# Five masked score levels of a gated linear-attention mixer, each computed as two 64-key halves instead of one 128-key product

## The chip, the cores and the metric

One NeuronCore of one Trainium2 chip runs the whole program. The metric is the device time of one execution in microseconds (us). Three executions of the kernel before took 3752.68, 3755.21 and 3758.10 us; their median, 3755.21 us, is the time before.

## What is computed

The program is a stack of four residual layers over 1024 tokens of 1024 channels. Only one part of the first layer matters here, its second mixer (a gated linear attention with 8 heads of 128 key and 128 value channels). Per head it computes, for gate decays `g` summed along the tokens:

```
g_c    = cumsum(log_f) within a chunk
scores = sum_d q[t,d] * k[s,d] * exp(g[t,d] - g[s,d])      for s <= t, else 0
out    = scores @ v + (q * exp(g)) @ state
state  = state * exp(g_end) + (k * exp(g_end - g))^T @ v
```

The reference uses chunks of 64 tokens; the kernel uses chunks of 128, which gives the same result. Before it stands a recurrent mixer, behind it an output projection, and behind that a second layer (a delta-rule recurrence) and two layers of attention, retention and pooling. None of them is touched.

## The kernel before, in words

`hgrn2` (from L529) runs the second mixer. All five engines run programs of their own and meet at semaphores. The work goes head by head: head 0, then a loop over heads 1 to 6, then head 7, all with the same `head` function on each engine.

**The levels.** `exp(g[t]-g[s])` can't be taken for a whole chunk as a product of a factor of t and a factor of s, for it would overflow. So the score matrix of a chunk (keys on the 128 partitions, queries along the free axis) is put together from five levels. For levels 0 to 3 the chunk is cut into blocks of 64, 32, 16 and 8 tokens (`HG_CROSS`), and the level holds the scores of keys in an even block with queries in the odd block right behind it, both decayed to the border between the two. Level 4 holds the scores inside blocks of 8 (`HG_DIAG`). Each level goes through four stations:

- `distance` (VectorE, L812 to L825): differences of `g` into `E`.
- `decays` (ScalarE, L704 to L712): exponentials of `E`.
- `decayed` (VectorE, L835/L837 for levels 0 to 3, L841/L842 for level 4 and for the state's operands): keys times decay into `ke`, queries times decay into `qe`. For levels 0 to 3 `qe` holds the queries of odd blocks alone, packed: 64 for each chunk. `ke` and `qe` have two buffers each, taken in turn.
- `level` (TensorE, L593 to L607): 8 float32 products, one for each chunk of 128 tokens, at L603. The stationary operand is the chunk's 128 keys of `ke`, the moving one the chunk's 64 packed queries (128 at level 4). The result goes to one PSUM bank per level (two at level 4, `B0`). A float32 product is two weight loads and two passes in the trace, so a level is 16 loads and 16 passes.
- `take_level` (VectorE, L851, L855): the scores that the level's mask marks are copied into `st`. Scores outside the mask are computed by the product and thrown away.

**The order on TensorE** within a head is written out by hand. The projections of the next head stand between the levels:

```
project_f(h+1); norm(h-1)
level(h,0); level(h,1)
project_q(h+1)
level(h,2); level(h,3)
project_g(h+1)
level(h,4); turn_k(h); state_steps(h)
project_v(h+1)
output(h)
```

`project_f`, `project_q` and `project_g` are 48 float16 products of 512 columns each (L142), `project_v` 192 of 128 columns (L157). `norm` (L637) sums squares of the previous head's output, `turn_k` (L613) transposes keys, `state_steps` (L621) forms what each chunk adds to the state, `output` (L629, L630) forms the head's output. `state_steps` waits for ScalarE's copy of the turned keys (L746) and for VectorE's take of level 4 (L855). `head(7)` has no projections, and `head(0)` has no norm of a head before it.

ScalarE takes in order: the decays of levels 0 and 1, `rstd(h-1)` (L716, L718, released by `norm`), the decays of level 2 (L704), `high_part(h-1)` (L722), `take_f(h+1)` (L679 with a table load, L680, and a weight split L109), a table load, the decays of level 3 (L704), then those of level 4 (L706 to L708) and of the state (L710 to L712), then `take_q(h+1)` (a table load and L686), `take_g(h+1)` (L690), the copy L746, `take_v(h+1)` (L694). `take_q` waits for VectorE to be done with the old queries (L907).

VectorE takes in order: the distances and decayed operands of levels 0 and 1, a copy of v (L885), take of level 0, the decayed operands of level 2, `normed(h-1)` (L860, L862), the distance of level 3, take of level 1, the decayed operands of level 3 (L835, L837), a low part (L868), the distances of level 4 and the state (L819 to L825), a weight split (L115), take of level 2, the decayed operands of level 4, take of level 3, the decayed operands of the state (L841, L842), `take_q` (L803), take of level 4 (L855), `take_g` (L807), the chain of states (L919, L922).

Of the kernel before, what the change touches and what calls it, by code (L numbers as in the profile page):

```python
# [130 lines left out]
def channel_major(pe, K, slot, rnd, u_hi, u_lo, banks, tile_ready=None):  # L131

    pe.wait_ge(K.w_full[slot], rnd + 2)
    w_hi = K.w_hi[:, slot, :].rearrange("p (k c) -> p k c", k=KT)
    w_lo = K.w_lo[:, slot, :].rearrange("p (k c) -> p k c", k=KT)
    for half, bank in enumerate(banks):
        cols = slice(half * HALF, (half + 1) * HALF)
        for k in range(KT):
            if half == 0 and tile_ready is not None:
                pe.wait_ge(tile_ready, k + 1)  # L140
            for n, (w, u) in enumerate(((w_hi, u_hi), (w_hi, u_lo), (w_lo, u_hi))):
                last = pe.matmul(K.psum[:, bank, :], w[:, k, :], u[:, k, cols],  # L142
                                 start=(k == 0 and n == 0), stop=(k == KT - 1 and n == 2))
    last.then_inc(K.w_free[slot], 1)


def token_major(pe, K, slot, rnd, u_hi, u_lo, banks):

    pe.wait_ge(K.w_full[slot], rnd + 2)
    w_hi = K.w_hi[:, slot, :].rearrange("p (k c) -> p k c", k=KT)  # L150
    w_lo = K.w_lo[:, slot, :].rearrange("p (k c) -> p k c", k=KT)
    for t in range(TT):
        toks = slice(t * P, (t + 1) * P)
        out = K.psum[:, banks[t // 4], (t % 4) * P:(t % 4 + 1) * P]
        for k in range(KT):
            for n, (w, u) in enumerate(((w_hi, u_hi), (w_hi, u_lo), (w_lo, u_hi))):
                last = pe.matmul(out, u[:, k, toks], w[:, k, :],  # L157
                                 start=(k == 0 and n == 0), stop=(k == KT - 1 and n == 2))
    last.then_inc(K.w_free[slot], 1)
# [369 lines left out]
def hgrn2(nc, K, A, first_round, ahead, spare):  # L529
# [7 lines left out]
    with nc.cleanup_on_exit(), ExitStack() as c:  # L537
# [7 lines left out]
        qe, ke = sb("qe", [P, 2, S]), sb("ke", [P, 2, S])  # L545
# [19 lines left out]
        A0, A1, B0, B1 = (K.bank_pair(n) for n in range(4))  # L565
        in_chunks = lambda x: x.rearrange("p (c t) -> p c t", c=NC)
        side = lambda x, n, late_side: x.rearrange("p (n a b) -> p n a b", a=2, b=HG_CROSS[n])[:, :, late_side, :]
        cross = lambda n: in_chunks(K.psum[:, 4 + n, :])
        later = lambda n: in_chunks(qe[:, n % 2, 0:S // 2])
        flat_states = states[:, :, :].rearrange("p c n -> p (c n)")  # L570

        with nc.Block() as block:
            @block.sync
            def _(sp):
                sp.dma_start(masks[:, :, :], A["c_hg_masks"]).then_inc(consts_in, 16)
                weight_loads(sp, K, first_round, H, lambda h: hgrn2_units(A, h), ahead)

            @block.tensor
            def _(pe):
                def project_f(h):  # L580
                    pe.wait_ge(g_taken, h + 1)
                    channel_major(pe, K, 0, h + first_round, K.u_hi, K.u_lo, (0, 1))

                def project_q(h):
                    pe.wait_ge(v_ready, h + 1)
                    channel_major(pe, K, 1, h + first_round, K.u_hi, K.u_lo, (2, 3))

                def project_g(h):
                    pe.wait_ge(f_ready, h + 1)
                    channel_major(pe, K, 2, h + first_round, K.u_hi, K.u_lo, (0, 1))  # L590

                def project_v(h):
                    pe.wait_ge(q_taken, h + 1)  # L593
                    token_major(pe, K, 3, h + first_round, K.u_hi, K.u_lo, (2, 3))

                def level(h, n):
                    pe.wait_ge(qk_ready, h * 6 + (n + 1))
                    if n == 2:
                        pe.wait_ge(rstd_ready, h + 1)
                    elif n == 4:  # L600
                        pe.wait_ge(level_taken, h * 5 + 2)
                    for ch in range(NC):
                        last = pe.matmul(cross(n)[:, ch, :] if n < 4 else in_chunks(B0)[:, ch, :],  # L603
                                         in_chunks(ke[:, n % 2, :])[:, ch, :],
                                         later(n)[:, ch, :] if n < 4 else in_chunks(qe[:, n % 2, :])[:, ch, :],
                                         start=True, stop=True)
                    last.then_inc(level_done, 1)  # L607

                def turn_k(h):
                    pe.wait_ge(qk_ready, h * 6 + 6)  # L610
                    pe.wait_ge(level_taken, h * 5 + 4)
                    for ch in range(NC):
                        last = pe.transpose(in_chunks(B1)[:, ch, :], in_chunks(ke[:, 1, :])[:, ch, :],  # L613
                                            K.ident[:, :])
                    last.then_inc(kt_done, 1)

                def state_steps(h):
                    pe.wait_ge(kt_ready, h + 1)
                    pe.wait_ge(level_taken, h * 5 + 5)
                    for ch in range(NC):  # L620
                        last = pe.matmul(in_chunks(B0)[:, ch, :], in_chunks(late[:, :])[:, ch, :],  # L621
                                         v[:, ch, :], start=True, stop=True)
                    last.then_inc(ds_done, 1)

                def output(h):
                    pe.wait_ge(state_ready, h + 1)
                    for ch in range(NC):
                        out = in_chunks(B1)[:, ch, :]
                        pe.matmul(out, v[:, ch, :], st[:, ch, :], start=True, stop=False)  # L629
                        last = pe.matmul(out, states[:, ch, :], in_chunks(qe[:, 1, :])[:, ch, :],  # L630
                                         start=False, stop=True)
                    last.then_inc(o_done, 1)

                def norm(h):
                    pe.wait_ge(o_ready, h + 1)
                    for half in range(2):
                        last = pe.matmul(B1[:, half * HALF:(half + 1) * HALF], K.ones[:, :],  # L637
                                         flat_states[:, half * HALF:(half + 1) * HALF], start=True, stop=True)
                    last.then_inc(norm_done, 1)

                def head(h, previous, following):
                    if following:
                        project_f(h + 1)
                    if previous:
                        norm(h - 1)
                    level(h, 0)
                    level(h, 1)
                    if following:
                        project_q(h + 1)
                    level(h, 2)  # L650
                    level(h, 3)
                    if following:
                        project_g(h + 1)
                    level(h, 4)
                    turn_k(h)
                    state_steps(h)
                    if following:
                        project_v(h + 1)
                    output(h)

                project_f(0)
                project_q(0)
                project_g(0)
                project_v(0)
                head(0, False, True)
                with pe.Fori(0, H - 2) as i:
                    head(i + 1, True, True)
                head(H - 1, True, False)
                norm(H - 1)
# [2524 lines left out]
```

## Time and profile before

| | |
|---|---|
| median of 3 executions | 3755.21 us |
| the profiled execution, its own time | 3758.37 us |
| its span in the trace | 3756.6 us |
| TensorE busy over the span | 90% (3394.3 us) |
| TensorE weight loads | 56% |
| VectorE, ScalarE, GpSimd busy | 50%, 37%, 15% |
| mean granted TensorE clock | 0.954 of full |
| the second mixer in the span | from about 320 to 839 us |
| busy time of L603 (the levels), 8 heads | 87.2 us of 640 passes |

In the profile PE is TensorE's matmul side, PEld its weight loads, DVE VectorE, ACT ScalarE. PEclk is the granted TensorE clock as a share of full speed: 1.00 is 2.4 GHz, 0.50 is 1.2 GHz. The shapes of a PE row are rows*columns of the array that the stationary operand takes, then the moving operand.

### The profile page before, as it was taken

The page shows a single profiled execution, that of the slowest core. Times are in us where ns is not written, and L with a number is a line of the kernel's source. Part 1 is how long each engine was busy: PE and PEld are TensorE (multiplying, and loading weights), DVE is VectorE, ACT ScalarE, POOL GpSimd, SP SyncE. Part 2 cuts the span into 40 slices and gives each one's busy share as a digit, 9 for nine tenths or more (in the row PEclk, how much of TensorE's full clock was granted, in tenths as well). Part 3 has the DMA queues.
Part 4 walks back from the last instruction along what each step waited for, and adds up shares of the span by engine and source line. Part 5 has one row for each costly group of instructions (what it writes and reads, how often), then busy time and mean ns, then how long its engine had stood idle before and what let it go on. Part 6 is the DMA issues. An engine that isn't in the chain of part 4 may idle for free. (4 is left out here: it accounts for less than half of the span.)

```text
span 3756.6 us, 74433 instructions
## 1 busy us (share of the span) xinstructions
PE 3394.3 (90%) x32138; PEld 2113.8 (56%) x32138; DVE 1872.9 (50%) x2563; ACT 1408.1 (37%) x2026; POOL 548.9 (15%) x350
## 2 busy tenths in 40 slices
PE   6887999969899898999998999979899999889889
PEld 3334766654444345888887457646544566657434
DVE  3654566653344724544554546654352366744342
ACT  3553354432355532323333435542311255523211
POOL 3000000002000002323332032300060133100330
PEclk8998999979999999999999999999999999999999
DMA  5101011103225643111110221011012111020121
GB/s 163 33 22 50 28 39 30 38 10 136 64 75 119 142 115 100 62 43 62 43 62 8 96 74 40 23 48 31 30 47 73 57 45 34 1 61 24 46 75 45
DMA packets 308334, 215.36 MB, mean 57 GB/s; under 512 B 125411, under 2 KB 283950, under 8 KB 305454
## 3 DMA queue, kind: packets, MB, share of 16 engines
q1 hardware_dynamic: 307608, 210.70, 18.7%
q8 instruction: 240, 3.93, 0.4%
q10 hardware_dynamic: 442, 0.37, 0.0%
q14 instruction: 44, 0.36, 0.0%
HBM read 173.26 MB, written 41.98 MB: 57 GB/s over the span
## 5 line engine op out<-in xcount | busy, mean ns | idle before, releaser
L142 PE MATMUL psum<-u,w_hi 128*128 128x512 f16 x2816 | 855.7, 386 | 103.1 <-DVEq L798 32.0
L142 PE MATMUL psum<-u,w_lo 128*128 128x512 f16 x1408 | 542.1, 385 | 0.0
L142 PEld LDWEIGHTS psum<-u,w_hi 128*128 128x128 f16 x2816 | 278.6, 100 | 452.6 <-issue 55.5
L97 POOL TENSOR_TENSOR w_hi<-stage,w_scale 128x1024 f16<-128x1024 f32 x52 | 99.4, 1912 | 1247.6 <-PE psum L142 604.8
L1063 PE MATMUL psum<-w_hi,merged 128*128 128x512 f16 x768 | 236.6, 390 | 25.0 <-PEq L2909 9.0
L115 DVE SCALAR_TENSOR_TENSOR w_lo<-stage,w_hi 128x1024 f16<-128x1024 f32 x124 | 149.1, 1219 | 184.6 <-ACT w_hi L109 184.5
L2497 DVE CUSTOM_DVE_ANT_0 probs_att<-psum,bias_att 128x1024 f32<-128x1024 f32 x128 | 156.7, 1224 | 168.3 <-PE psum L2309 167.5
L2287 PE MATMUL psum<-u,w_hi 128*128 128x512 f16 x768 | 231.7, 384 | 6.7 <-PEq L966 6.7
L142 PEld LDWEIGHTS psum<-u,w_lo 128*128 128x128 f16 x1408 | 139.8, 99 | 172.6 <-issue 11.5
L1063 PE MATMUL psum<-held_hi_out,merged 128*128 128x512 f16 x768 | 231.1, 379 | 0.0
L157 PE MATMUL psum<-w_hi,u 128*128 128x128 f16 x2048 | 173.2, 219 | 0.0
L157 PE MATMUL psum<-w_lo,u 128*128 128x128 f16 x1024 | 172.3, 219 | 0.0
L2119 DVE COPY_PREDICATED Tt_rc<-tmask_rc,psum 128x256 f32<-128x256 uint32 x192 | 83.4, 443 | 173.7 <-PE psum L1804 156.0
L142 PE MATMUL psum<-mix_b_rp,w_hi 128*128 128x512 f16 x512 | 153.7, 382 | 11.3 <-DVE mix_b_rp L1569 10.8
L157 PEld LDWEIGHTS psum<-w_hi,u 128*128 128x128 f16 x2048 | 157.9, 98 | 4.9 <-issue 4.6
L2406 ACT ACTIVATE probs_att<-probs_att,neg_max_att 128x1024 f32<-128x1024 f32 x128 | 146.3, 1146 | 19.6 <-DVE neg_max_att L2501 19.4
L2337 PE MATMUL psum<-turned_att,merged 128*128 128x128 f32 x1024 | 139.7, 281 | 15.0 <-ACT sq_att L2420 14.6
L1063 PE MATMUL psum<-w_lo,merged 128*128 128x512 f16 x384 | 149.6, 390 | 0.0
L2337 PEld LDWEIGHTS psum<-turned_att,merged 128*128 128x128 f32 x1024 | 132.4, 195 | 27.7 <-issue 17.7
L109 ACT ACTIVATE w_hi<-stage 128x1024 f16<-128x1024 f32 x124 | 127.6, 1048 | 52.1 <-PE psum L1063 41.2
L1063 PEld LDWEIGHTS psum<-w_hi,merged 128*128 128x128 f16 x768 | 76.8, 100 | 124.7 <-issue 38.8
L2287 PE MATMUL psum<-u,w_lo 128*128 128x512 f16 x384 | 146.8, 382 | 0.0
(446 smaller groups left out, 6842.2 us busy)
## 6 DMA issues: line engine op xcount, KB each, us to landing
stage<-w_in SPq DMA_DIRECT2D x72, 512.0 KB, 3.8
X<-rwkv_chunks SPq DMA_DIRECT2D x14, 1792.0 KB, 8.4
stage<-ab_w_in SPq DMA_DIRECT2D x48, 512.0 KB, 4.9
stage<-rw_w_in SPq DMA_DIRECT2D x32, 512.0 KB, 4.4
rwkv_chunks<-work_rp SPq DMA_DIRECT2D x26, 512.0 KB, 5.7
stage<-w_out SPq DMA_DIRECT2D x24, 512.0 KB, 5.8
X<-x SPq DMA_DIRECT2D x16, 512.0 KB, 10.8
stage<-ab_w_out SPq DMA_DIRECT2D x16, 512.0 KB, 5.5
```

Of the source, the lines that this page charges most:

```text
L97: pool.tensor_tensor(K.w_hi[:, slot, :], K.stage[:, slot, :], scale, ALU.mult).then_inc(K.w_half[slot], 1)
L109: act.mul(K.w_hi[:, slot, :], K.stage[:, slot, :], W_SCALE).then_inc(K.w_half[slot], 1)
L115: dve.scalar_tensor_tensor(K.w_lo[:, slot, :], K.stage[:, slot, :], W_SCALE, K.w_hi[:, slot, :], ALU.mult, ALU.subtract).then_inc(K.w_full ...
L142: last = pe.matmul(K.psum[:, bank, :], w[:, k, :], u[:, k, cols], start=(k == 0 and n == 0), stop=(k == KT - 1 and n == 2))
L157: last = pe.matmul(out, u[:, k, toks], w[:, k, :], start=(k == 0 and n == 0), stop=(k == KT - 1 and n == 2))
L1063: last = pe.matmul(bank_of(half, t), m[:, 2 * u + k, toks(t)], w[:, at, w_cols], start=(u == 0 and k == 0 and n == 0), stop=(u == UH - 1 a ...
L2119: dve.copy_predicated(Tt[:, q, g * GJ:g * GJ + GJ], mask, data).then_inc(t_ready, 1)
L2287: last = pe.matmul(K.psum[:, PROJ + half, :], w[:, kt, :], u[:, kt, cols(half)], start=(kt == 0 and n == 0), stop=(kt == KT - 1 and n == 2))
L2337: last = pe.matmul(K.psum[:, O_BANK, (i % 4) * P:(i % 4 + 1) * P], v_tiles[h % 2][:, half * 4 + n, :], turned[:, half, n, :], start=(half ...
L2406: act.activation(probs[:, s % 2, m, :], probs[:, s % 2, m, :], ACT.Exp, bias=neg_max[:, s % 2, m:m + 1], accum_out=sums[:, s % 2, m:m + 1] ...
L2497: dve.tensor_tensor_reduce(probs[:, s % 2, m, :], K.bank_pair(m), bias[:, h % 2, at:at + S], LOGIT_UNSCALE, LOWEST, ALU.add, ALU.max, neg_ ...
```

## The change

Only `level` on TensorE changes. Level 0 multiplies the first 64 keys of a chunk alone (the later 64 are in no even block of 64 tokens) with the chunk's 64 packed queries, into PSUM partitions 0 to 63. Levels 1 to 3 become two products for each chunk: keys 0 to 63 with the first 32 packed queries into partitions 0 to 63, and keys 64 to 127 with the last 32 packed queries into partitions 64 to 127. Level 4 becomes two products as well, 64 keys with the 64 queries of their own half. Banks, masks, semaphores and everything on the other engines stay. The numbers of products are 8, 16, 16, 16, 16 where they were 8 in each level.

```
@@ def level(h, n) @@
+                    keys = in_chunks(ke[:, n % 2, :])
+                    queries, out = (later(n), cross(n)) if n < 4 else (in_chunks(qe[:, 0, :]), in_chunks(B0))
                     for ch in range(NC):
-                        last = pe.matmul(cross(n)[:, ch, :] if n < 4 else in_chunks(B0)[:, ch, :],
-                                         in_chunks(ke[:, n % 2, :])[:, ch, :],
-                                         later(n)[:, ch, :] if n < 4 else in_chunks(qe[:, n % 2, :])[:, ch, :],
-                                         start=True, stop=True)
+                        if n == 0:
+                            last = pe.matmul(out[0:64, ch, :], keys[:, ch, 0:64], queries[:, ch, :],
+                                             start=True, stop=True)
+                            continue
+                        width = 32 if n < 4 else 64
+                        for side_of in range(2):
+                            at, cols = slice(64 * side_of, 64 * side_of + 64), slice(width * side_of,
+                                                                                    width * side_of + width)
+                            last = pe.matmul(out[at, ch, cols], keys[:, ch, at], queries[:, ch, cols],
+                                             start=True, stop=True)
                     last.then_inc(level_done, 1)
```

## Rows read from the trace of the kernel before

**Rows 1.** Heads 3, 5, 7: length; busy PE, PEld, DVE, ACT, POOL; PEclk; DMA; GB/s

```profile
533.20:594.40 61.20, 59.10 (x479) 41.01 (x477) 38.80 (x50) 29.35 (x30) 0.00 (x0) 1.00 0.12 34
655.60:718.00 62.40, 60.64 (x478) 41.82 (x476) 38.76 (x50) 29.34 (x30) 0.00 (x0) 0.97 0.11 34
779.30:840.00 60.70, 31.63 (x147) 27.02 (x146) 37.75 (x48) 23.86 (x25) 0.00 (x0) 0.68 0.00 0
```

**Rows 2.** TensorE in head 3, in order of time: start, length, work, idle before

```profile
543.54 1.88 PE L637 MATMUL psum<-states_hg,ones 128*128 128x512 f32 x4
545.25 3.68 PE L603 MATMUL psum<-qe_hg,ke_hg 128*128 128x64 f32 x32
...
559.13 1.90 PE L603 MATMUL psum<-qe_hg,ke_hg 128*128 128x64 f32 x16
561.61 2.00 PE L603 MATMUL psum<-qe_hg,ke_hg 128*128 128x64 f32 x16 [0.58 <-DVE qe_hg L837]
573.80 1.95 PE L603 MATMUL psum<-qe_hg,ke_hg 128*128 128x128 f32 x16
575.59 1.04 PE L613 MATMUL psum<-ident,ke_hg 128*128 128x128 f32 x8
578.14 2.05 PE L621 MATMUL psum<-v_hg,room 128*128 128x128 f32 x16 [1.51 <-DVE st_hg L855]
```

**Rows 3.** ScalarE in head 3, in order of time

```profile
545.45 1.11 ACT L716 ACTIVATE states_hg<-psum,eps 128x1024 f32<-128x1024 f32 x1 [1.40 <-PE psum L637]
...
559.17 1.06 ACT L704 ACTIVATE E_hg<-E_hg 128x1024 f32<-128x1024 f32 x1
...
573.27 1.28 ACT L686 ACT_TABLE_LOAD   x1 [4.29 <-DVEq L907]
574.57 1.02 ACT L686 ACTIVATE X<-psum 128x1024 f32<-128x1024 f32 x1
...
576.66 1.01 ACT L746 COPY room<-psum 128x1024 f32<-128x1024 f32 x1 [0.16 <-PE psum L613]
```

**Rows 4.** VectorE in head 3, in order of time

```profile
548.67 0.69 DVE L835 TENSOR_TENSOR ke_hg<-X,E_hg 128x512 f32<-128x512 f32 x1 [0.62 <-ACT E_hg L704]
...
560.26 0.69 DVE L835 TENSOR_TENSOR ke_hg<-X,E_hg 128x512 f32<-128x512 f32 x1 [5.17 <-ACT E_hg L704]
...
571.93 1.22 DVE L842 TENSOR_TENSOR qe_hg<-X,states_hg 128x1024 f32<-128x1024 f32 x1
575.62 1.22 DVE L803 SCALAR_TENSOR_TENSOR X<-psum,X 128x1024 f32<-128x1024 f32 x1 [2.48 <-ACT X L686]
576.76 1.32 DVE L855 COPY_PREDICATED st_hg<-room,psum 128x1024 f32<-128x1024 uint32 x1
```

**Rows 5.** TensorE with 64-column operands elsewhere, in order of time, and a change of shape

```profile
1501.28 0.33 PE L1815 MATMUL psum<-Hs_rc,ar_rc 64*64 64x64 f32 x4
1501.39 0.33 PE L1814 MATMUL psum<-vT_rc,ak_rc 64*64 64x64 f32 x4
...
1502.91 0.33 PE L1815 MATMUL psum<-Hs_rc,ar_rc 64*64 64x64 f32 x4
1503.17 1.12 PE L1772 MATMUL psum<-bon_rc,pair_ones 128*128 128x512 f32 x2
1504.23 0.45 PE L1826 MATMUL psum<-u,Tt_rc 64*64 64x64 f32 x8
```

**Rows 6.** TensorE in head 0, in order of time

```profile
359.15 2.17 PE L603 MATMUL psum<-qe_hg,ke_hg 128*128 128x64 f32 x16 [2.36 <-DVE qe_hg L837]
361.74 3.68 PE L603 MATMUL psum<-qe_hg,ke_hg 128*128 128x64 f32 x16 [0.42 <-DVE qe_hg L837]
...
376.78 3.68 PE L603 MATMUL psum<-qe_hg,ke_hg 128*128 128x64 f32 x32
```

**Rows 7.** VectorE in head 7: the two takes that wait for a level

```profile
794.19 0.73 DVE L851 COPY_PREDICATED st_hg<-room,psum 128x512 f32<-128x512 uint32 x1 [0.70 <-PE psum L603]
...
814.79 1.33 DVE L855 COPY_PREDICATED st_hg<-room,psum 128x1024 f32<-128x1024 uint32 x1 [0.81 <-PE psum L603]
```

## The prediction

> **What bounds the kernel now.** I read three views: the stretches by head, each engine's order of time inside one head, and the groups by shape. The stretches show a head taking 61.2 us with TensorE busy for 59.1 of them [rows 1]. That looks like a kernel bound by TensorE, from which every shortened product would be a gain. The order of time says otherwise, and it decides the forecast.
>
> In head 3 TensorE ends `norm` as level 0 begins at 545.25 (two pairs of `norm` passes lie before it, 543.54 on). ScalarE takes the result at 545.45 [rows 2, 3]. From there a chain runs over ScalarE and VectorE alone: `rstd`, the decays of level 2, VectorE's operands of level 2 at 548.67, `normed`, then ScalarE's `high_part`, two table loads, `take_f` and a weight split, the decays of level 3 at 559.17, VectorE's operands of level 3 at 560.26 to 561.55, its unbroken work down to the state's operands (571.93 to 573.15), ScalarE's table load at 573.27 and sigmoid at 574.57, VectorE's L803 at 575.62 and the take of level 4, 576.76 to 578.08 [rows 3, 4]. `state_steps` starts at 578.14, released by that take [rows 2]. Not one link of the chain waits for a level: VectorE idles before L835 for the exponential both times (0.62 and 5.17 us), ScalarE before the table load for VectorE (4.29 us). So 578.14 - 545.25 = 32.9 us of the head are set by ScalarE and VectorE. TensorE's part of the period is the rest: `state_steps`, `project_v`, `output`, `project_f` and `norm`, 61.2 - 32.9 = 28.3 us. The levels lie in the 32.9 us, beside the chain. TensorE waits twice there, 0.58 us before level 3 and 1.51 us before `state_steps` [rows 2].
>
> Heads 1 to 6 are built so. Head 5 took 62.4 us instead of 61.2 at a mean clock of 0.97 [rows 1]: 0.03 x 62.4 / 0.5 = 3.7 us at 1.2 GHz, half of which is 1.9 us of array time. It cost 1.2. A delay of TensorE beside the chain is taken up to the slack, and the slack is small: `turn_k` ends at 576.63, ScalarE's copy runs 576.66 to 577.67, `state_steps` starts at 578.14, so some 0.45 us [rows 2, 3].
>
> **The change, step by step.** *What a level costs.* Level 3 (64 moving columns) and level 4 (128) both take 16 load-and-pass pairs; their groups last 2.00 and 1.95 us [rows 2], of which 0.16 us is the last pass running out, so 0.112 us a pair at either width. The moving columns cost nothing; the 128-column load sets the pace. Halving the moving columns alone therefore saves nothing. The halved load saves only if the doubled number of loads runs side by side.
>
> *Bounds of a new level.* Upper, for tiles in turn: levels 1 to 4 issue 32 pairs with 64-column loads at 0.056 us, 1.8 us, as now. Level 0 (16 pairs) takes 0.9. Lower, for the two halves side by side: the nearest rows are the 64x64 products of the second layer, which alternate between halves of the array, four passes every 0.117 us (1501.28, 1501.39, ..., 1502.91), that is 0.029 us a pair [rows 5]. 32 pairs are then 0.93 us and every level is 0.93. Those rows use different rows of the array as well as different columns; here both halves use all 128 rows, so the lower bound isn't shown. I take it, because the order is the same (two passes for one half, two for the other) and these are the nearest rows; the upper bound stays for the range.
>
> *Changes of shape.* Each block of levels is entered from 128-column work and left to it: six changes per head. From 64 to 128 columns, the next pass was due at 1502.91 + 0.117 = 1503.03 and came at 1503.17: 0.14 us. Back, two passes of 0.43 us from 1503.17 are through at 1504.03 and the next came at 1504.23: 0.20 us [rows 5]. I take 0.17 each. The Trainium skill ("TensorEngine Tiling (Array Packing)", Key Properties) says that a change of tiling mode drains TensorE; the trace agrees, at those 0.14 to 0.20 us.
>
> *Heads 1 to 6.* Level 0 shorter by 0.9: level 1 still waits for its operands, which VectorE finishes at 546.8, so `project_q` starts at 546.8 + 0.93 + 0.17 = 547.9 instead of 548.8, 0.9 us earlier. Level 2, 0.17 later for the change and 0.87 shorter, ends 1.6 us earlier; level 3 waits for the operands ready at 561.55 as before, and the idle time before it grows from 0.58 to about 2.2 us. Level 3, `project_g`, level 4 and `turn_k` then end 2 x 0.87 less 3 x 0.17, 1.2 us, earlier; `state_steps` stays at 578.14 and the idle time before it grows from 1.51 to 2.7 us. Gain: 0. If the halves run in turn: three changes of shape, 0.5 us, against a slack of 0.45: 0 to 0.1 us a head lost. Cover: the 32.9 us chain. Were it gone, the five levels would be worth 5 x 0.87 less six changes, 1.0, so 3.3 us a head.
>
> *Head 0* has no `norm` chain and TensorE is behind all along. Level 1 starts at 361.74, gated by its operands, at 1.2 GHz: 3.5 us become 1.9, less a change, 1.4; the products behind it run at the same clock, so half of it counts, 0.7. Levels 2 and 3 run without a gap, 3.52 us up to the next work [rows 6]; they become 1.86, and level 4 saves 0.87. Less four more changes, 0.7. Sum 0.7 + 1.66 + 0.87 - 0.7 = 2.5 us. In turn: nothing saved, 0.8 lost.
>
> *Head 7* runs its levels at 1.2 GHz (mean 0.68 over the stretch [rows 1]). VectorE waits 0.70 us for level 0 and 0.81 us for level 4 [rows 7]; the first wait goes in either case, of the second 0.3 to 0.5, as `turn_k` and the copy follow. But the array works less before `state_steps` there, and the clock may return later. I take 0.5, with -1.2 and +1.2 as ends.
>
> *Head 5's* 1.2 us would fall under the grown slack. Against that stands the longer idle time elsewhere: in head 0 the array stood idle for 2.36 us and the narrow levels behind it ran at the low clock [rows 6]. Idle times of 2.2 and 2.7 us in each head will bring such falls. One that hits `project_g` is paid out of the slack of 1.7 us; one that hits `state_steps` and `project_v` is on the path and costs about what half of head 5's 3.7 us is, up to 1.9 us. I count one such head, 1.2 against 1.2: zero.
>
> Sum: -2.5 - 0.5 = -3.0 us, or +0.3 if the halves go in turn. The profiled execution's own time is 3758.37 (span 3756.6 and 1.8 around it), so 3755.4; it stood 3.2 us above the median of 3755.21, so 3752.2 against the median. About 0.2%, 7.5 us, is what a measurement of this kernel can tell from no change.
>
> **Rivals.** (a) *Loads and passes of one row group don't overlap* (slower). The Trainium skill ("TensorE: Matmul & The Clock Gate", Part 3, What overlaps and what doesn't) says a weight load overlaps passes in flight only when the row groups differ, and both halves here use all rows. Rows 2 speak against it: level 4's pairs take 0.112 us, though a pass of 128 columns, a quarter of `norm`'s 0.43 us, is 0.107 and the load that sets level 3's pace 0.112: the two overlap on the same rows. But that is shown for full-width operands only. If a half-width pair did go one after the other: load 0.056 plus pass 0.027 (32 columns) or 0.054 (64), so 2.7 us for levels 1 to 3 and 3.5 for level 4. Levels 1 and 2 then push level 3 by 0.9 + 0.9, three changes by 0.5, less 0.58 of idle time, 1.7 us; level 3 adds 0.9, level 4 1.7, the changes 0.5, less 0.45 of slack: 4.3 us a head, six heads, and about 8 in the others: +34, 3789. It decides from the point where a level exceeds about 2 us. Chance 0.06.
> (b) *The clock.* More idle time lets the clock fall where it is on the path, in most heads rather than one. For it: head 0's row, and that the narrow levels keep the array less busy. Against: `project_v` and `output` are dense, and the 1.51 us idle in each head caused nothing now. Seven heads at 1.9 us less the 3 gained: +10, 3765. Chance 0.09.
> (c) *The levels count in full*: 6 x 3.3 + 3 = 23 us, 3732. Against it the chain above. Chance 0.04.
> (d) *In turn*: the change brings no shorter level, 3755.5. Chance 0.28.
> Forecast 0.53.
>
> **The numbers.** Forecast and (d) both lie within 0.2%: 0.81; 0.02 of it goes to a forecast that turns out faster by more: same 0.79. Faster 0.04 + 0.02 = 0.06, slower (a) and (b), 0.15. The range runs from 3747 (the forecast with the gains of heads 5 and 7 in full and nothing lost to the clock) to 3764, which takes in (d) and most of (b), and leaves out (a) and (c).
>
> **What would show it.** Right: L603's groups at about 0.93 us a level, the idle time before level 3 near 2.2 us and before `state_steps` near 2.7, still released by L837 and L855, the period at 61.2. If a level is 1.8 us, (d). If it exceeds 2.5 us and `state_steps` is released by the copy L746, (a). A PEclk under 1.00 in several heads with periods above 62 is (b). A period under 60.5 us would refute the chain.

## The result, and the profile after

The changed kernel takes 3771.17 us (median of 5 executions, 3766.04 to 3773.99). Beside it on the same chip the kernel before took 3755.21 us (5 executions, 3749.53 to 3760.34). The ratio is 1.0041, 95% interval 1.0026 to 1.0056: slower, above the predicted range of 3747 to 3764 us. The profiled execution's own time is 3771.17 us, its span 3769.4.

The page of the changed kernel, its head and the busy times of the engines:

```profile
span 3769.4 us, 75457 instructions
...
PE 3379.0 (90%) x32650; PEld 2083.6 (55%) x32650; DVE 1872.4 (50%) x2563; ACT 1408.0 (37%) x2026; POOL 548.9 (15%) x350
```

TensorE is busy 15.3 us less than before (3394.3) and the span is 12.8 us longer. The levels (L603 before, L606 for level 0 and L613 for the others now), groups kept apart by shape: passes, busy us and mean ns of one, idle time before them:

```profile
L613 PE MATMUL psum<-qe_hg,ke_hg 128*64 128x32 f32 x768 | 31.6, 242 | 22.4 <-DVE qe_hg L845 22.4
...
L613 PE MATMUL psum<-qe_hg,ke_hg 128*64 128x64 f32 x256 | 10.0, 237 | 5.9 <-DVE qe_hg L850 5.9
L606 PE MATMUL psum<-qe_hg,ke_hg 128*64 128x64 f32 x128 | 10.0, 236 | 6.0 <-DVE qe_hg L845 6.0
```

Together 51.6 us busy where it was 87.2. So the levels did become shorter. TensorE in head 3, in order of time; these lines answer to [rows 2]:

```profile
543.12 1.14 PE L606 MATMUL psum<-qe_hg,ke_hg 128*64 128x64 f32 x16
544.61 1.13 PE L613 MATMUL psum<-qe_hg,ke_hg 128*64 128x32 f32 x32 [0.34 <-DVE qe_hg L845]
...
556.13 1.12 PE L613 MATMUL psum<-qe_hg,ke_hg 128*64 128x32 f32 x32
559.38 1.12 PE L613 MATMUL psum<-qe_hg,ke_hg 128*64 128x32 f32 x32 [2.13 <-DVE qe_hg L845]
...
570.91 1.15 PE L613 MATMUL psum<-qe_hg,ke_hg 128*64 128x64 f32 x32
571.99 1.09 PE L621 MATMUL psum<-ident,ke_hg 128*128 128x128 f32 x8
575.92 3.79 PE L629 MATMUL psum<-v_hg,room 128*128 128x128 f32 x16 [2.84 <-DVE st_hg L863]
579.50 0.42 PE L157 MATMUL psum<-w_hi,u 128*128 128x128 f16 x2
```

The 32 pairs of a load and a pass of levels 1 to 4 take 1.12 to 1.15 us; less the 0.16 us of the last pass running out that is some 0.96, where 16 pairs took 1.84. Level 0 has 16 pairs, all in one half of the array, and takes 1.14 us, no less: 0.061 us a pair with one half alone against 0.030 with both. The time went into waiting: 2.13 us before level 3 (0.58 before) and 2.84 us before `state_steps` (1.51), released by the same two lines as before. And the last two rows have something that was not there: `state_steps`, all of it 128-column work that the change doesn't touch, takes 3.79 us instead of 2.05, and `project_v` behind it starts 3.58 us after it, where in the kernel before it was 1.89:

```profile
580.03 0.28 PE L157 MATMUL psum<-w_hi,u 128*128 128x128 f16 x2
```

Stretches of the changed kernel (columns as in [rows 1]): head 3, then head 4 with its tail, then the falls of the clock: two stretches from 575.00 on (just ahead of `state_steps` of head 3), one in head 4, one from 762.80 on (just ahead of `state_steps` of head 6) and the long one in head 7:

```profile
530.90:592.10 61.20, 55.89 (x517) 36.67 (x517) 37.42 (x48) 26.41 (x27) 0.00 (x0) 0.94 0.12 34
592.10:656.60 64.50, 60.85 (x561) 40.06 (x560) 39.47 (x50) 31.47 (x32) 0.00 (x0) 0.95 0.11 33
575.00:578.40 3.40, 2.48 (x11) 2.48 (x12) 2.11 (x3) 0.19 (x1) 0.00 (x0) 0.51 0.00 0
578.40:581.80 3.40, 3.40 (x29) 3.34 (x28) 1.68 (x5) 0.00 (x0) 0.00 (x0) 0.50 0.00 0
622.80:629.60 6.80, 6.18 (x43) 3.37 (x44) 6.65 (x8) 2.93 (x3) 0.00 (x0) 0.50 0.00 0
762.80:766.20 3.40, 2.54 (x12) 2.54 (x13) 2.04 (x3) 0.13 (x1) 0.00 (x0) 0.50 0.00 0
793.50:824.20 30.70, 15.45 (x168) 13.98 (x168) 23.53 (x31) 11.63 (x13) 0.00 (x0) 0.50 0.00 1
```

The last five stretches ran at 1.2 GHz. The fall at 575.0 comes in the widened idle time before `state_steps` and lasts through it into `project_v`.

**Where the 12.8 us of span came from.** I cut both traces at the same instructions. Up to the second mixer's first work (at 296.3 us in the kernel before, not at 320): -0.6 us. The second mixer: 543.45 us before, 550.17 after, +6.7. From there to the delta-rule stage of the second layer: no difference. That stage's loop, from its first product (L1753 before, L1761 after) to its end: 594.28 before, 601.70 after, **+7.4, in code that the change doesn't touch**. Everything behind: -0.7 us.

The loop as one stretch, first the kernel before, then the changed kernel:

```profile
1468.09:2062.37 594.28, 544.21 (x14368) 493.88 (x14368) 302.86 (x568) 187.03 (x411) 185.72 (x170) 0.96 0.13 47
```

```profile
1474.19:2075.89 601.70, 545.44 (x14368) 492.93 (x14368) 302.03 (x568) 187.00 (x411) 185.83 (x170) 0.96 0.13 46
```

The same counts, the same busy times within 1.3 us on every engine, the same mean clock. TensorE's idle time, the length less its busy time, grew from 50.1 to 56.3 us. The waits of TensorE in that loop (line waited for, releaser; us in total, times, longest), before and then after; "issue" means that nothing the profile shows held TensorE up:

```profile
PE psum L1753 <- issue: 16.9, 5, 3.5
...
PE psum L1800 <- issue: 9.8, 7, 2.3
...
PE psum L1788 <- issue: 1.9, 1, 1.9
...
PE psum L1804 <- issue: 1.1, 2, 0.6
```

```profile
PE psum L1761 <- issue: 21.0, 5, 4.3
...
PE psum L1812 <- issue: 8.6, 11, 1.2
...
PE psum L1808 <- issue: 5.4, 6, 2.6
...
PE psum L1786 <- issue: 1.0, 4, 0.4
```

29.7 us became 36.0: 6.3 of the 7.4 us are waits for which the profile shows no cause. The lines have also traded places: the wait that L1800 (now L1808) had is smaller, and L1804 (now L1812) has eleven where it had two short ones. In the timeline such a stop stands between the last products of one chunk and the first ones of the next, in the changed kernel:

```profile
1912.05 1.25 PE L1808 MATMUL psum<-u,T_rc 64*64 64x64 f32 x32
1917.50 3.68 PE L1761 MATMUL psum<-ar_rc,bt_rc 64*64 64x128 f32 x32 [4.20 <-issue]
```

The five stops at L1753 have a place of their own. The loop of the program (`Fori` at L1708) runs two chunks a turn, six turns, with two chunks' first products ahead of it and two behind. In the kernel before, the stops come 136.8, 211.0, 288.8, 362.7 and 434.9 us after the first product: every second chunk, each time right behind the jump back to the loop's start (the branch instruction stands in the trace 3.7 to 4.1 us ahead of the product that waited). The sixth turn, which doesn't jump back, has none. All fourteen traces below have these five stops, at the same turns. The stops of about 1 us at the other lines stand in code without a jump.

### The profile page after: what moved, and what is told of

The parts are those of the page before. It is cut to its first block and busy times, and to the rows that moved or that the text cites. A ratio compares the mean times of both kernels' runs of the same rounds, so it can differ in the third digit from the quotient of the medians.

```text
span 3769.4 us, 75457 instructions
## 1 busy us (share of the span) xinstructions
PE 3379.0 (90%) x32650; PEld 2083.6 (55%) x32650; DVE 1872.4 (50%) x2563; ACT 1408.0 (37%) x2026; POOL 548.9 (15%) x350
## 5 line engine op out<-in xcount | busy, mean ns | idle before, releaser
L142 PE MATMUL psum<-mix_b_rp,w_hi 128*128 128x512 f16 x512 | 153.8, 382 | 11.9 <-DVE mix_b_rp L1577 11.4
L109 ACT ACTIVATE w_hi<-stage 128x1024 f16<-128x1024 f32 x124 | 127.6, 1048 | 51.6 <-PE psum L1071 40.7
```

The source lines that it names most:

```text
L109: act.mul(K.w_hi[:, slot, :], K.stage[:, slot, :], W_SCALE).then_inc(K.w_half[slot], 1)
```

## The experiments

Two theories had to be told apart for each half of the loss. For the mixer: **the clock** (the array works less, idle times are longer, the clock falls in stretches that count) against **the shape** (two column halves or the changes of shape hold up the work behind them). For the loop: **the place of the code** (TensorE's program in front of the loop grew, so the loop lies elsewhere against the borders at which instructions are fetched) against **an effect of the mixer** (a later start, other data, another state of the chip) or chance.

A float32 product is four instructions of TensorE, and the body of a head stands in the program three times (head 0, the loop, head 7). With 32 products more in each, the loop lies 32 x 4 x 3 = 384 instructions further on. I call this its **shift**.

**1. `after_again`, the changed kernel again**, no edit.

> The changed kernel once more, to see what of its trace repeats. Clock theory (the shorter levels lengthen TensorE's idle times, the clock falls to 1.2 GHz more often in the second mixer and partly on the path): 3766 to 3774 us, the mixer (its start to its end) again some 5 to 9 us longer than before, with four or more stretches of heads 1 to 6 at a clock under 1.00, at other heads than last time perhaps. Chance theory (the difference came from where the clock fell behind the mixer, in the second layer): the second layer takes 606 us again instead of 613.6, and the total is 3760 to 3766.

Measured: 3772.14 us (3770.0 to 3781.68, 6 executions), ratio 1.0047, 1.0035 to 1.0059. Second mixer 550.13, loop 601.16: inside the range of the clock theory. The `state_steps` of the eight heads follow one another at the same seven distances, to 0.03 us. The falls of the clock in the mixer are not chance: the same program has them in the same places.

**2. `filled`**, the changed kernel with the array kept busy in heads 1 to 6: level 2 is computed three times, level 4 and `turn_k` twice.

```
-                for ch in range(NC):
+                for ch in [c for _ in range(times) for c in range(NC)]:
...
+                    middle = previous and following
-                    level(h, 2)
+                    level(h, 2, 3 if middle else 1)
...
-                    level(h, 4)
-                    turn_k(h)
+                    level(h, 4, 2 if middle else 1)
+                    turn_k(h, 2 if middle else 1)
```

> The changed kernel with more array work in heads 1 to 6: level 2 is issued three times, level 4 and the turning of the keys twice, with the semaphore on the last; results are the same. The idle times of TensorE are then again about 0.6 us before level 3 and 1.5 us before the state's products. Clock theory: more work makes it faster, heads 1 to 6 take 61.2 us each with hardly a fall of the clock, head 0 keeps its 3.5 us: 3749 to 3757 us. Shape theory (the changes between 128- and 64-column tiles or the narrow products themselves cost): as slow as the changed kernel or slower, 3770 to 3776.

Measured: 3767.03 us (3764.36 to 3769.97, 6 executions), ratio 1.0031, 1.0019 to 1.0043. Second mixer 543.88 us, 6.3 less than the changed kernel takes, with more work. The total misses the clock theory's 3749 to 3757. Two heads of it (columns as above):

```profile
528.40:589.70 61.30, 59.52 (x646) 40.33 (x645) 38.80 (x49) 29.30 (x30) 0.00 (x0) 1.00 0.12 34
589.70:651.10 61.40, 59.62 (x647) 40.42 (x647) 38.80 (x49) 29.40 (x30) 0.00 (x0) 1.00 0.12 34
```

and `state_steps` of head 3 in its timeline:

```profile
575.52 2.05 PE L629 MATMUL psum<-v_hg,room 128*128 128x128 f32 x16 [1.18 <-ACT room L755]
```

The clock does not fall in heads 1 to 6, every one of them takes 61.35 us, and `state_steps` is back at 2.05 us. The half-width products and their changes of shape are all there. The shape theory falls, and for heads 1 to 6 the clock theory stands. Head 7 was not filled, and its long fall is even longer here, 44.4 us from 780.3 on: from its `state_steps` until the last `norm` is done it takes 18.6 us, where it took 14.4 before and takes 17.6 in the changed kernel. That is why the mixer comes back to 543.9 and not to the 539.5 that the gain of head 0 would give. The whole stays 11 us above the kernel before because the loop of the second layer, at 601.34 us, did not come back with the mixer: that loss is another one.

**3. `half_count`**, the kernel before with its full 128-key products, but only 4 for each level (it leaves out half of the scores), so that TensorE has as little to do as in the changed kernel.

```
-                    for ch in range(NC):
...
+                    for ch in range(0, NC, 2):
+                        if n < 4:
+                            out = K.psum[:, 4 + n, ch * 64:ch * 64 + 128]
+                            queries = qe[:, n % 2, ch * 64:ch * 64 + 128]
+                        else:
+                            out, queries = in_chunks(B0)[:, ch, :], in_chunks(qe[:, 0, :])[:, ch, :]
+                        last = pe.matmul(out, in_chunks(ke[:, n % 2, :])[:, ch, :], queries, start=True, stop=True)
```

> The kernel before, with 128-key products throughout, but only four of the eight products in each level: it leaves out half of the score products (levels 0 to 3 multiply the keys of even chunks with the queries of two chunks, level 4 does even chunks alone). A level takes the same 0.9 us as in the changed kernel, without any 64-column tile. Clock theory: the same falls of the clock and the same loss as the changed kernel, 3763 to 3775 us. Shape theory: nothing is lost, and head 0 gains: 3749 to 3755.

Measured: 3771.03 us (3766.09 to 3772.86, 5 executions), ratio 1.0037, 1.0024 to 1.005. By its total this kernel looks like the changed one and seems to prove the clock theory. The parts say otherwise: its second mixer takes 539.58 us, 3.9 less than before, and its loop takes 610.81, 16.5 more. The total is near for a wrong reason. Two heads and one fall:

```profile
526.30:587.50 61.20, 56.73 (x438) 37.38 (x437) 38.79 (x49) 29.36 (x30) 0.00 (x0) 0.97 0.12 34
587.50:648.60 61.10, 56.66 (x438) 37.15 (x437) 38.79 (x49) 29.27 (x30) 0.00 (x0) 0.97 0.12 34
557.80:561.20 3.40, 3.40 (x12) 1.75 (x12) 3.25 (x4) 0.71 (x1) 0.00 (x0) 0.51 0.00 0
```

The array's work per head is as low as in the changed kernel (56.7 us against 55.9) and the clock does fall, once in each of heads 1 to 6 for 3.4 us. But it falls each time at level 3, beside the chain, and costs nothing: the heads take 61.2 us. Less work alone is thus not enough for a loss; the fall must hit work that sets the end. And the loop of the second layer, longer again after a change in front of it (240 instructions fewer), was the hint to the place of the code.

**4. `head0_only`**: halves in head 0 alone, where the prediction saw nearly all the gain; heads 1 to 7 as before.

```
-                def level(h, n):
+                def level(h, n, halves):
...
+                        if not halves:
+                            last = pe.matmul(out[:, ch, :], keys[:, ch, :], queries[:, ch, :], start=True, stop=True)
+                            continue
...
-                    level(h, 0)
+                    level(h, 0, not previous)
```

> The two-half products in head 0 alone, the 128-key products in heads 1 to 7. Clock theory: head 0 keeps its gain of about 3.5 us, heads 1 to 7 are as before: 3749 to 3754 us, the fastest of all. Shape theory: head 0 alone pays 6 of 48 changes, 3753 to 3758.

Measured: 3758.97 us (3752.32 to 3764.99, 11 executions), ratio 1.0007, 0.9999 to 1.0016. The total misses the clock theory's 3749 to 3754. Second mixer 539.45 us, 4.0 less than before; the clock does not fall in heads 1 to 6 and all of them take 61.2 us, so head 5's 1.3 us is gained too. Loop 604.89 us, 10.6 more than before (shift 128): the gain is real and is lost again 600 us later.

**5 to 8. Moving the loop alone.** 128 or 256 semaphore increments on TensorE, right ahead of the second-layer stage. They compute nothing and wait for nothing; the kernels are the one before, the changed one and `head0_only`.

```
             @block.tensor
             def _(pe):
+                for _ in range(128):
+                    pe.sem_inc(seen, 1)
```

> The kernel before with 128 semaphore increments (0.05 us each) put ahead of the second layer's loop in TensorE's program, at a place where TensorE waits some 16 us anyway. Nothing else changes. Code-place theory (the second layer's loop is longer than the instruction store, is fetched again in 16 KB blocks in every pass, and where the block borders fall in it decides how long TensorE stands at them; the changed kernel moved that loop by 384 instructions, which is 128 beyond a whole block of 256): the second layer's stage takes 613 to 617 us instead of 606, the mixer is untouched at 543.5, total 3762 to 3768 us. Clock theory (all of the loss comes from falls of the clock that the shorter levels cause): 3752 to 3760, as the kernel before.

> The same with 256 increments, one whole block of 16 KB at 64 bytes an instruction. Code-place theory: the borders fall where they fell in the kernel before, so the stage takes 606 us again and the total is 3753 to 3759. If the added instructions themselves cost something, this kernel is slower than the one with 128. Clock theory: 3752 to 3760.

> The changed kernel with 128 increments at that place: its loop then lies 512 instructions, two whole blocks, behind where it lay before. Code-place theory: the second layer's stage is back at 606 us, the mixer stays at 550, total 3761 to 3766 us, 6 to 10 less than the changed kernel. Clock theory: unchanged, 3768 to 3775.

> Two-half products in head 0 alone, with 128 increments: the loop lies one whole block behind its old place. Code-place theory: mixer 539.5, second layer's stage 606, total 3749 to 3755 us, faster than both kernels. Clock theory: as without the increments, 3755 to 3762.

Measured: `before_pad128` 3776.5 us (ratio 1.0056, 1.0043 to 1.0069), `before_pad256` 3783.49 (1.0076, 1.0063 to 1.0089), `after_pad128` 3768.48 (1.0035, 1.0023 to 1.0047), `head0_pad128` 3761.16 (1.0014, 1.0006 to 1.0023). All four totals missed, because an increment costs some 0.15 us, not the 0.05 I had counted: TensorE's idle time before the loop's first product grew from 15.8 us to 24.3 with 128 and to 44.0 with 256. Two of them, `after_pad128` and `head0_pad128`, even fall into the range of the clock theory, so the totals decide nothing here.

```profile
1475.44 3.68 PE L1756 MATMUL psum<-ar_rc,bt_rc 64*64 64x128 f32 x32 [24.30 <-issue]
```

The parts are clear. The loop takes 606.58 us in `before_pad128`, and 590.21, 592.10 and 592.63 in the other three. The changed kernel's loop, 601.70, becomes 9.6 us shorter by 128 instructions that do nothing, and that of the kernel before grows by 12.3 with them and shrinks back with 128 more.

**9 to 12. The same increments where TensorE stands idle**, at the end of its program for the recurrent mixer (the array is idle there from 270.7 us on, until the second mixer), so that they cost nothing.

```
+        spare = sem("spare")
...
+                for _ in range(128):
+                    pe.sem_inc(spare, 1)
```

> The kernel before with 128 semaphore increments at the end of the first mixer's TensorE program, where TensorE stands idle for 28 us (267 to 295.6), so that their 20 us cost nothing. Code-place theory, cleanly: mixer 543, the second layer's loop 601 to 607 us instead of 594, total 3761 to 3770 us. Clock theory: 3752 to 3760.

> The changed kernel with the same 128 increments: its second-layer loop lies two whole blocks behind the old place. This is the change with the place of the code taken out. Code-place theory with the clock theory for the mixer: mixer 550, loop 590 to 594, total 3757 to 3763 us, so 2 to 7 above the kernel before and 10 to 14 under the changed one. Clock theory alone: 3768 to 3775.

> Halves in head 0 alone, with the same 128 increments (one whole block). Mixer 539.5, loop 590 to 594: 3748 to 3754 us, faster than the kernel before by 2 to 6 us. If the increments in the first mixer cost something, up to 3758.

> Halves in head 0 alone, with 64 increments: the loop lies 192 instructions beyond its old place, a place not seen so far. Code-place theory gives no number for a new place beyond what was seen, loop 590 to 611, and so 3748 to 3770 us; it expects stops at other products of the loop than at shifts 0 and 128. Mixer 539.5 in any case.

Measured, against 3755.3 us of the kernel before in these rounds (21 executions):

| kernel | us | executions | ratio, 95% interval |
|---|---|---|---|
| before, +128 | 3768.2 | 5 | 1.0037, 1.0023 to 1.005 |
| changed, +128 | 3760.88 | 11 | 1.0015, 1.0006 to 1.0024 |
| `head0_only`, +128 | 3750.63 | 11 | 0.9988, 0.9979 to 0.9997 |
| `head0_only`, +64 | 3784.91 | 5 | 1.0075, 1.0061 to 1.0089 |

The first three totals lie in the ranges of the code-place theory. The fourth lies 15 us above the range that was given for a place not seen before.

The first row is the cleanest of all: a kernel with exactly the arithmetic and order of the one before is 13 us slower. Its second mixer takes 543.20 us, as before. Its loop, in the view of stretches, and the waits of TensorE there:

```profile
1468.49:2076.74 608.25, 547.11 (x14368) 493.85 (x14368) 301.36 (x568) 187.01 (x411) 185.91 (x170) 0.96 0.13 46
```

```profile
PE psum L1756 <- issue: 22.3, 5, 4.6
...
PE psum L1807 <- issue: 12.1, 11, 1.5
...
PE psum L1803 <- issue: 4.9, 6, 2.6
```

It is the changed kernel's pattern (its lines are 3 further on than in the kernel before, 5 less than in the changed one): five stops at a chunk's first products, eleven at L1804 of before, six of up to 2.6 us at L1800. The changed kernel with 128 increments (11 lines further on) is back near the pattern of the kernel before, five, six and one stop at L1753, L1800 and L1788, and of the eleven five short ones are left:

```profile
PE psum L1764 <- issue: 18.6, 5, 3.8
...
PE psum L1811 <- issue: 7.2, 6, 1.7
PE psum L1799 <- issue: 1.9, 1, 1.9
PE psum L1815 <- issue: 1.9, 5, 0.5
```

and `head0_only` with 64 instead of 128 (14 lines further on) has one of its own, with eight stops at L1788 of before, up to 3.6 us each:

```profile
PE psum L1802 <- issue: 19.2, 8, 3.6
PE psum L1767 <- issue: 17.4, 5, 3.7
```

All fourteen traces, by the remainder of the shift over 256 instructions:

| shift, of 256 | loop of the second layer, us | of it TensorE idle, us | of it at 1.2 GHz, us | kernels |
|---|---|---|---|---|
| 0 | 594.3, 590.2, 592.1, 590.0, 592.6, 592.3 | 49.2 to 52.2 | 29 to 45 | before; before +256; changed +128 (late, early); `head0_only` +128 (late, early) |
| 16 | 610.8 | 58.9 | 65 | `half_count` |
| 80 | 601.3 | 57.1 | 45 | `filled` |
| 128 | 601.7, 601.2, 604.9, 606.6, 608.3 | 55.9 to 61.7 | 40 to 49 | changed, twice; `head0_only`; before +128 (late, early) |
| 192 | 629.9 | 72.1 | 67 | `head0_only` +64 |

Six traces, with three different mixers and with starts of the loop from 1463 to 1496 us, lie within 4.3 us at shift 0; none of the other eight is within 6 us of them. What stands in front of the loop doesn't matter, only how many instructions it is. An effect of the mixer is thereby ruled out. The clock is not what tells the places apart, but it adds to them. TensorE's idle time parts them cleanly: the worst trace at shift 0 has 52.2 us, the best of all others 55.9. The time at 1.2 GHz overlaps, and on the whole it is longer where the loop is idle more. Take the changed kernel and its copy with 128 early increments: of the 11.8 us between their loops 6.0 are idle time and 5.8 busy time, and 48.7 us against 33.6 ran at 1.2 GHz. So at equal shift, too, single traces differ by the clock: the kernel before and `before_pad256` have 50.1 and 49.2 us of idle time, but 44.7 and 37.2 us at 1.2 GHz, and that is most of the 4.1 us between them. The kernel before happened to lie in the best place that I found.

Why 256? The trace shows that the loop's instructions are fetched while it runs. The DMA queue of instructions within the loop, kernel before, and within 410 to 760 us, where the loop over the heads runs; packets, MB and share of 16 engines:

```profile
q8 instruction: 123, 2.02, 1.4%
```

```profile
q8 instruction: 4, 0.07, 0.1%
```

2.02 MB in 123 packets are 16 KB each, and 14368 loads and 14368 passes are 28736 instructions, 112 times 256: about one fetch for each 256 instructions, every time round. The heads' loop is hardly fetched anew. The Trainium skill ("Runtime: NRT & Kernel Launch", Instruction fetch mechanics) gives the block of a fetch as 16 KiB, 256 instructions, and says that crossing into the next is mostly hidden while a taken branch out of the window stalls. The five long stops behind the jump back agree with that. What the page doesn't tell is that their length depends on the place: 3.2 to 3.8 us each at shifts 0, 16 and 192, 4.1 to 5.0 at 80 and 128. And "mostly hidden" leaves out the other stops, of 0.3 to 3.6 us at lines without a jump (L1800, L1804 and L1788), which come and go with the shift. The number of fetched packets is 123 in the changed kernel as well, so not how much is fetched changes. That it is where in the work the borders fall is the reading that fits a period of 256; no trace shows which stop belongs to which border.

## Why the prediction was wrong, and where it was right

**What a level costs: right.** Some 0.96 us for levels 1 to 4 where the forecast took 0.93 and rival (d) 1.8, and 0.98 for level 0. The lower bound, which the rows of before showed only for operands in different rows of the array, holds for two column halves of all 128 rows. Rivals (a) and (d) fall. The Trainium skill ("TensorE: Matmul & The Clock Gate", Part 3, What overlaps and what doesn't) lets a load overlap only passes of another row group; the measured 0.030 us a pair on the same rows, half of the 0.061 that a pair takes where one half works alone, does not agree, and the measurement decides.

**The chain of ScalarE and VectorE: right.** In the changed kernel four of the distances from one head's `state_steps` to the next are 61.20 to 61.22 us; in head 3 idle time before level 3 is 2.13 (2.2 forecast), before `state_steps` 2.84 (2.7), the releasers as named. Rival (c) falls: 35.6 us less busy time of the levels bought nothing in six heads of eight.

**Head 0: right.** 2.9 us gained where 2.5 were forecast (`state_steps` starts 3.6 us earlier, of which 0.6 to 0.7 came from an earlier start of the second mixer).

**The clock, first error: a term of the sum that was mis-sized.** The step is "I count one such head, 1.2 against 1.2: zero", with "up to 1.9 us" as the price of a fall on the path. What the runs showed is two such heads (3 and 6) at 2.8 us each, two more (1 and 4) at 1.3 each for a fall beside the chain, head 5's 1.3 gained, and 3.2 lost at the end in head 7: some +10 us where the sum had zero. With the gains of 2.9 in head 0 and 0.4 in head 7 that makes the mixer's +6.8. The distances between `state_steps` of heads 0 to 7, kernel before: 61.2 four times, 62.5 once (head 5's loss), 61.2, then 53.7. Changed: 62.49, 61.22, 61.20, 65.31, 61.22, 61.20, 56.10. Laid against each other:

| where | us | what the rows show |
|---|---|---|
| head 0 | -2.9 | shorter levels |
| head 1 | +1.3 | 6.8 us at 1.2 GHz from 435.1, beside the chain but longer than its slack |
| head 3 to 4 | +4.1 | falls at 575.0 and 622.8 |
| head 5 | -1.3 | the loss of before is gone |
| head 6 to 7 | +2.4 | fall at 762.8, less what shorter levels gain |
| behind head 7's `state_steps` | +3.2 | the long fall begins later against the work |
| sum | +6.8 | the second mixer: +6.7 |

The 4.1 us taken apart: from its start to that of `project_v` `state_steps` takes 3.58 for 1.89 us, and `project_v` 12.02 for 10.88, together 2.8. The other 1.3 come from the fall at 622.8, which makes `turn_k` late, so that head 4's `state_steps` waits for ScalarE's copy, no longer for VectorE's take:

```profile
641.23 0.48 PE L629 MATMUL psum<-v_hg,room 128*128 128x128 f32 x2 [1.18 <-ACT room L754]
```

So a fall beside the chain costs nothing (the two of 3.4 us, from 499.9 and 687.7) or 1.3 us (the two of 6.8 us, and head 5's of 3.4 us before, where the slack was small). One on the path costs 2.8, not "up to 1.9": that figure was half of head 5's 3.7 us, and these falls last 6.8 us, with 1.7 us of loss in `state_steps` alone. Head 6's comes out the same, 2.8, less 0.4 that shorter levels gain in head 7. In head 7 the prediction gave 0.5 us of gain with 1.2 us of loss as the end. The long fall of 30.7 us was there before as well, from 784.1, 21.0 us behind head 6's `state_steps`:

```profile
784.10:814.80 30.70, 19.93 (x85) 17.98 (x84) 27.40 (x34) 11.40 (x13) 0.00 (x0) 0.50 0.00 1
```

It ended at 814.8, ahead of head 7's `state_steps` at 816.8. In the changed kernel it lies at 793.5, 29.8 us behind head 6's, ends at 824.2, and covers `state_steps`:

```profile
819.75 3.78 PE L629 MATMUL psum<-v_hg,room 128*128 128x128 f32 x16 [1.10 <-ACT room L754]
```

The stretch from the start of head 7's `state_steps` until the last `norm` is done is the longer the further the long fall reaches into it: 14.4 us in the kernel before (the fall ends 2.0 us ahead of `state_steps`), 16.0 in `half_count` (3.1 behind it), 17.6 in the changed kernel (4.4 behind), 18.6 in `filled` (11.9 behind).

This is rival (b). For heads 1 to 6 its mechanism is shown by `filled`, which takes the falls away and with them the loss, and by the repeated run; for head 7 no run takes the fall away, and the 3.78 us of its `state_steps` and the four stretches above are what speaks for it. It struck not in most heads, as (b) had it, but in few, and harder. Where the falls land is the same in all four traces that have the changed mixer (changed, repeated, and the two with increments), but I can't derive the places from the change; half-width levels in head 0 alone brought no such fall.

**The loop of the second layer, second error: a step that is missing.** The sum took everything outside the second mixer as unchanged. It is unchanged in what it computes and in what order, but TensorE's program in front of it had grown by 384 instructions, 128 of 256, and that cost 7.4 us. The rows that the prediction rests on end with the second mixer, but for [rows 5]; the waits of L1753 and L1800 on "issue" and the 123 instruction packets were in the trace of before, and no term was made of them. No rival had it.

**What the change is worth with the second error taken out**: changed +128 early against before, both at shift 0, is 3760.88 us, ratio 1.0015 (1.0006 to 1.0024), 5.6 us slower. Its second mixer takes 550.10 us, 6.7 more than before. That is the clock's loss, and it puts the change on the side of rival (b), not of the forecast. The two traces don't add up to the 5.6 stage by stage: the loop is 4.3 us shorter in the one of the changed kernel, for the trace of the kernel before has the longest loop of the six at shift 0, and its execution lies 3 us above its median. And the gain of head 0, with the loop left in its place, is a version that beats both: 3750.63 us, 0.9988 (0.9979 to 0.9997).

**Open.** Why shifts 16 and 192 cost more than 80 and 128: only one trace each, and no run tells which stop is due to which block border. Whether the stops are what brings the low clock in the loop. And whether falls could be moved off the path by a filling placed at just those two waits; `filled` did it with more work than needed, and at a cost of 0.15 us a head.

## What to carry to other kernels

Where another pair of engines sets the period, shorter array work buys only idle time, and idle time is not free: it can bring the clock down in the work behind it, so price each fall on the path with what dense work loses in it (2.8 us for 6.8 us at 1.2 GHz here), not with zero, and read the granted clock of the stretch after each wait. A change that adds or removes instructions ahead of a loop that is fetched anew each time round (read the instruction queue's packets in its stretch) also moves that loop; before a difference under 1% is put down to the edit, cut both traces into stages, look whether untouched stages moved, and time both kernels with the loop at the same place, by adding instructions that do nothing where the engine is idle. A total that agrees with the expectation proves little until its parts do.

## What the runs showed of the hardware that was not expected

- **The place of a long loop in TensorE's program is worth up to 40 us of 590** (590.0 at shift 0, 629.9 at shift 192), with equal counts and busy times of the other engines within 6 us. Of these 40 us 22 are idle time of TensorE, which stands in the profile as waits on "issue" of up to 5.0 us each; the other 18 are busy time, with 67 us at 1.2 GHz against 34.
- **A jump back in that loop stops TensorE for 3.2 to 5.0 us**, five times in every trace: 3.2 to 3.8 each at shifts 0, 16 and 192, 4.1 to 5.0 at 80 and 128.
- **A semaphore increment on TensorE costs about 0.15 us of its time**: (44.0 - 24.3) / 128 = 0.154. The profile gives each a length of 0.05 us.
- **Two 64-column halves with all 128 rows run side by side**: 32 pairs of loads and passes in 0.96 us, 0.030 us a pair, against 0.061 with one half alone (level 0) and 0.112 for a 128-column pair.
- **The falls of the clock repeat**: four traces on separate executions have them within 0.03 us of one another, as measured by the distances of `state_steps`.
